# Modulation columns in the dense products: scaled by ScalarE and added up by GpSimd instead of summed by VectorE

## The reference, cut to what matters

```python
c_act = jax.nn.silu(c)
mod = c_act @ ada_w[layer] + ada_b[layer]          # (1, 2048) @ (2048, 6 * 2048)
sh1, sc1, g1, sh2, sc2, g2 = [m[:, None, :] for m in jnp.split(mod, 6, axis=-1)]
u = rms_norm(h, norm_mix_g[layer]) * (1.0 + sc1) + sh1
h = h + g1 * hybrid_mixer(u, ...)
u = rms_norm(h, norm_ffn_g[layer]) * (1.0 + sc2) + sh2
h = h + g2 * swiglu(u, ...)
```

## The kernel before, in words

| product | turns x groups | chunks of modulation columns a turn |
|---|---|---|
| in_1 | 8 x 8 | 1 |
| out_1 | 2 x 8 | 1 |
| ff_1 | 8 x 8 | 1 |
| ff_2 | 4 x 16 | 3 |
| out_2 | 2 x 8 | 2 |
| gate_up | 11 x 8 | 1, in its first 4 turns |
| down | 2 x 22 | none |

## Time and profile before

### The profile page before, as it was taken

The page is one execution under the profiler, slowest core; times in us unless marked ns, Lnnn a source line. Parts: engine busy times, 40 slices in busy tenths (PEclk is TensorE's granted clock), DMA queues, the critical chain, the costliest instruction groups (busy, mean ns, idle before and its releaser), DMA issues. The chain is left out here.

```text
span 3280.2 us, 57828 instructions
## 1 busy us (share of the span) xinstructions
PE 2891.9 (88%) x22235; PEld 2786.1 (85%) x22235; DVE 2000.5 (61%) x2742; ACT 1378.5 (42%) x2121; POOL 314.9 (10%) x427
## 2 busy tenths in 40 slices
PE   2399999769788999999999699999798999999998
PEld 2399998748788999988889588888688999999997
DVE  6856556746556666587788534545577654445664
ACT  1234334252434444444444334545434444444554
POOL 2011112600001111111111000000111100000000
PEclk6699999679898999999999788999999999999999
DMA  9688896110355877687788252324576765555553
GB/s 341 212 246 243 234 245 174 65 39 1 136 172 197 286 258 272 232 286 264 264 276 272 69 148 93 118 91 128 193 257 236 263 212 174 190 181 167 187 174 114
DMA packets 295455, 632.09 MB, mean 193 GB/s; under 512 B 23746, under 2 KB 44678, under 8 KB 295046
## 3 DMA queue, kind: packets, MB, share of 16 engines
q1 hardware_dynamic: 240080, 467.97, 44.5%
q0 software_dynamic: 43776, 159.40, 14.0%
q10 hardware_dynamic: 11446, 2.54, 0.5%
HBM read 627.77 MB, written 2.10 MB: 192 GB/s over the span
## 5 line engine op out<-in xcount | busy, mean ns | idle before, releaser
L741 PE MATMUL accumulators<-h_parts,weight_parts 128*128 128x256 f32 x5696 | 1454.7, 287 | 28.1 <-DVE weight_parts L679 27.9
L743 PE MATMUL accumulators<-h_parts,weight_parts 128*128 128x256 f32 x5696 | 1443.7, 285 | 0.0
L679 DVE TENSOR_TENSOR weight_parts<-weights,weight_parts 128x1024 fp32r<-128x1024 f32 (+1 forms) x840 | 877.6, 1058 | 532.8 <-ACT weight_parts L642 531.7
L741 PEld LDWEIGHTS accumulators<-h_parts,weight_parts 128*128 128x128 f32 x5696 | 1106.8, 194 | 44.6 <-DVE weight_parts L679 41.2
L743 PEld LDWEIGHTS accumulators<-h_parts,weight_parts 128*128 128x128 f32 x5696 | 1107.9, 195 | 0.0
L642 ACT ACTIVATE weight_parts<-weights 128x1024 fp32r<-128x1024 f32 (+1 forms) x840 | 747.3, 920 | 750.1 <-DMA weights<-in_w_in 201.9
L734 PE MATMUL accumulators<-h_parts,weight_parts 128*128 128x256 f32 x5696 | 935.6, 287 | 112.2 <-DVE h_parts L668 61.0
L734 PEld LDWEIGHTS accumulators<-h_parts,weight_parts 128*128 128x128 f32 x5696 | 798.0, 195 | 122.7 <-issue 89.3
L641 ACT ACTIVATE h_parts<-wide 128x512 fp32r<-128x512 f32 x216 | 135.6, 628 | 355.8 <-DMA weights<-in_w_ff 199.7
L362 DVE SCALAR_TENSOR_TENSOR ada_sums<-ada_weights,c_act,ada_sums 128x512 f32<-128x512 f32 x392 | 278.1, 746 | 0.0
L2177 DVE TENSOR_TENSOR in_weight_parts<-weights,in_weight_parts 128x512 fp32r<-128x512 f32 (+6 forms) x224 | 130.8, 597 | 209.2 <-ACT in_weight_parts L1964 208.1
(11 more groups left out here) (321 smaller groups left out, 1864.2 us busy)
## 6 DMA issues: line engine op xcount, KB each, us to landing
weights<-in_w_ff SPq DMA_DIRECT2D x128, 1024.0 KB, 6.5
weights<-in_w_in SPq DMA_DIRECT2D x80, 1024.0 KB, 8.1
h_t<-in_ada_w POOLq DMA_DIRECT2D x128, 512.0 KB, 5.9
ada_weights<-in_w_ada POOLq DMA_DIRECT2D x96, 512.0 KB, 6.2
weights<-in_ffn_w_gate SPq DMA_DIRECT2D x44, 1024.0 KB, 5.2
weights<-in_ffn_w_up SPq DMA_DIRECT2D x44, 1024.0 KB, 5.1
weights<-in_ffn_w_down SPq DMA_DIRECT2D x44, 1024.0 KB, 5.0
ada_weights<-in_w_ada SPq DMA_DIRECT2D x64, 512.0 KB, 8.2
```

The lines of the kernel that those rows point to most:

```text
L679: ins = nc.vector.tensor_tensor(w[:, held:held + take, 1, :], core.ring[:, q % RING, k:k + take, :], w[:, held:held + take, 0, :].bitcast( ...
L741: nc.tensor.matmul(accs[nt], w[:, held, 0, cols[nt]], xk[:, 1, :], start=False, stop=False, skip_group_check=True)
L743: ins = nc.tensor.matmul(accs[nt], w[:, held, 1, cols[nt]], xk[:, 0, :], start=False, stop=(last and nt % 2 == 1), skip_group_check=True)
```

## The change

`Ada.step` is used no longer in the dense products, only in the first phase. In its place ScalarE scales each row tile of columns, by one activation with the number as its scale (`Ada.scale`): the first two of a chunk into the two sums, the other 14 in place in the ring. The steps are placed behind ScalarE's high parts by the formula that placed them behind VectorE's low parts. GpSimd adds the 14 scaled tiles to the two sums in turn, then the sums to one another, and issues the loads in between, each when the slot has been added up (`Ada.loads_and_sums`). ScalarE's queue now holds the waits for landed columns and for taken sums. TensorE waits for the same semaphore `ada_sums_ready`, which GpSimd raises.

```diff
+    def scale(self, act, i, s):
+        nc, core, n = self.nc, self.core, self.per_turn
+        c, k = s // KT, s % KT
+        which = self.parts[c][1]
+        if s == 0:
+            act.wait_ge(core.ada_sums_taken, i * n + (self.chunks0 + 1))
+        q = c * AGROUPS + k // AK
+        if k % AK == 0:
+            act.wait_ge(self.landed[q % self.slots],
+                        i * (16 * self.per_slot) + 16 * (self.landed0 + q // self.slots + 1))
+        w = self.ring[:, q % self.slots, k % AK, :]
+        nc.scalar.activation(self.acc[:, c, k, :] if k < 2 else w, w, ACT.Copy,
+                             scale=core.c_act[:, KT * which + k:KT * which + k + 1]).then_inc(core.ada_scaled, 1)
+
+    def loads_and_sums(self, pool):
+        nc, core = self.nc, self.core
+        self.first_loads(pool)
+        chunks = self.turns * self.per_turn
+        for chunk in range(chunks):
+            acc = self.acc[:, chunk % self.per_turn]
+            scaled, added = self.scaled0 + KT * chunk, self.added0 + (KT - 1) * chunk
+            for k in range(KT):
+                w = self.ring[:, (chunk * AGROUPS + k // AK) % self.slots, k % AK, :]
+                pool.wait_ge(core.ada_scaled, scaled + k + 1)
+                if k >= 2:
+                    if k >= 4:
+                        pool.wait_ge(core.ada_added, added + k - 3)
+                    nc.gpsimd.tensor_tensor(acc[:, k % 2, :], acc[:, k % 2, :], w, ALU.add
+                                            ).then_inc(core.ada_added, 1)
+                load = chunk * AGROUPS + k // AK + self.slots
+                if k % AK == AK - 1 and load < chunks * AGROUPS:
+                    pool.wait_ge(core.ada_added, added + max(k - 1, 0))
+                    self.load(pool, load // (self.per_turn * AGROUPS), load % (self.per_turn * AGROUPS))
+            pool.wait_ge(core.ada_added, added + KT - 2)
+            nc.gpsimd.tensor_tensor(acc[:, 0, :], acc[:, 0, :], acc[:, 1, :], ALU.add).then_inc(core.ada_added, 1)
+            pool.wait_ge(core.ada_added, added + KT - 1)
+            pool.sem_inc(core.ada_sums_ready, 1)
...
                     nc.scalar.activation(w[:, held:held + take, 0, :], core.ring[:, q % RING, k:k + take, :], ACT.Copy
                                          ).then_inc(core.high_ready, take)
+                    if with_sums and 0 < q < st.unit - 1:
+                        n, slots, at = ada.per_turn * KT, KG * (st.unit - 2) // take, (KG * (q - 1) + k) // take
+                        for s in range(n * at // slots, n * (at + 1) // slots):
+                            ada.scale(act, i, s)
...
-                    if with_sums and 0 < q < st.unit - 1:
-                        n, slots, at = ada.per_turn * KT, KG * (st.unit - 2) // take, (KG * (q - 1) + k) // take
-                        for s in range(n * at // slots, n * (at + 1) // slots):
-                            ada.step(dve, i, s)
...
-                ada.first_loads(pool)
-                ada.other_loads(pool)
+                ada.loads_and_sums(pool)
```

51 lines of the change are left out of this document (28 added, 23 removed).

## The result

The changed kernel takes **3463.53 us** (median of 4 runs, 3457.72 to 3468.19), the kernel before 3285.14 us (4 runs, 3277.24 to 3285.92): ratio 1.0548, 95% interval 1.0522 to 1.0574, 178 us slower. The forecast was 3375 us with a range of 3300 to 3460. The direction was right, the size was not: the loss is about twice the forecast, and the time is 3.5 us above the range. The profiled execution took 3468.19 us, its span 3466.5 us, at a mean granted clock of 0.914 (before 0.929).

A forecast was written before the change was run, and what follows sets the result against it. TensorE was taken to bound ff_1 and gate_up, late weight loads behind VectorE's work ff_2. Terms of +46, +26, +12, +6 and +3 gave +93 on 3281.9, so 3375 us, range 3300 to 3460.

The forecast's parts named there:

- What bounds the kernel: TensorE alone in ff_1 and gate_up; in ff_2, weight loads that start late behind VectorE's low parts and sums.
- The loop of the earlier trace: In ff_2, weights landing, last low part (6.5 us), next load landing (7.2 us): 13.7 us for two groups, sums inside.
- Prices: Assumed costs per operation: ScalarE scaling 0.71 us, GpSimd addition 1.2 us, between 1.13 and 1.43.
- dear additions: Rival: GpSimd additions cost 1.43 us each, so late columns stop ScalarE and TensorE; +197 us, 3479 us, chance 0.12.
- The ring turns faster: Rival: no holding, additions at 1.13 us, weight loads start sooner in ff_2 and in_1; −16 us, 3266 us, chance 0.07.
- GpSimd yields: Rival: VectorE keeps the shared SBUF access and GpSimd waits without holding it; +30 us, 3312 us, chance 0.17.
- Held both ways: Claim that GpSimd's additions and VectorE's two-operand low parts each wait for the other's whole instruction on SBUF.
- Term 1, ff_2: Low parts and additions exclude each other, making a turn 119 us instead of 107.5; +46 us, ends −13 to +102.
- Term 2, out_2: GpSimd needs 58 us a turn against TensorE's 46.2, so TensorE waits for sums; +26 us, ends +7 to +40.
- Term 3, in_1: Held low parts lengthen the loop 0.6 us a group, partly made up by a shorter DMA queue; +12 us.
- Term 4, ff_1: VectorE's 5.3 us a group fits under TensorE's 5.77, except after relu steps; +6 us, ends 0 to +20.
- Term 5, out_1 and gate_up: Same shape as ff_1, in six turns; +3 us, ends 0 to +10.

The follow-up runs named there:

- e9: Kernel before, with VectorE's sum steps behind the group's last low part only in ff_2 and out_2: 3240.15 us, ratio 0.9879.
- e1: Changed kernel without GpSimd's additions, sums left out, ScalarE still scaling: 3284.51 us, ratio 1.0030 to the kernel before.
- e3: Changed kernel with each GpSimd addition replaced by a one-operand product by 1.0, sums left out: 3479.4 us, a single run.
- e2: Changed kernel with each GpSimd addition replaced by two fills that only write, sums left out: 3360.42 us, ratio 1.0241 to the kernel before.
- e10: Changed kernel with write-only fills for GpSimd's additions and TensorE's partition sums after the turn's last group: 3309.50 us, ratio 1.0074 to the kernel before.
- e4: Changed kernel with TensorE's partition sums after the turn's last group instead of ahead of it: 3422.84 us, ratio 1.0453 to the kernel before.
- e5: Changed kernel with each GpSimd addition waiting for the one just before it, opening gaps: 3470.35 us, ratio 1.0570 to the kernel before.
- e6: Changed kernel with VectorE making the additions at its old steps' places, GpSimd only loading: 3285.02 us, ratio 1.0009 to the kernel before.

## Why the prediction was right in kind and too small

**What bounds the kernel: right.** The loop of the earlier trace rows is real: e9 shortens it and gains 35 us in ff_2, if partly by faster loads. ff_1 and gate_up were covered by TensorE, and e1 shows that VectorE's freed time is worth nothing there.

**Prices: right.** Scaling 0.709 us (0.71 said). Addition 1.25 us alone, 1.31 at the median (1.2 taken, 1.13 to 1.43 as ends). The *dear additions* rival gave 3479 us, nearest to the measured 3463.5, but its cause did not occur: an addition by itself cost 1.25 us, not 1.43. That its time fits is luck. *The ring turns faster* fell with the low parts' means. *GpSimd yields* did not occur with the additions of the change; e3 shows it for another form.

**Held both ways: right.** Low parts of 128x1024 were to be about 1.8 us in mean with a minimum of 1.22; in ff_2 the mean is 1.98, over all stages 1.68. Additions that met one took up to 2.4 us, as said.

**Term 1, ff_2: slightly too small.** +61 for +46, within its ends. e2 and the changed kernel, 443.5 and 500.4 us, put 57 us on the held access; without holding ff_2 was to get shorter by 13, and e1 shows 6. What the term left out is in the last paragraphs of this section.

**Term 2, out_2: right.** +31 for +26. In the first turn TensorE waited 9.6 us for GpSimd's closing addition, as forecast; in the second it was stopped by the low part that eight additions held, before it came to the sums. e10 and e2 show a loss of the same order (+21, +38) with nothing held.

**Term 3, in_1: the first step that failed.** I took +12 of a computed +29, on the ground that part of a late start is made up by a shorter DMA queue. Measured: +40. Two things were wrong. The loop grew by more than the 1.2 us that I had computed (two slots share it, which gives the 0.6 us a group): from the first high part to the last low part, in groups with sums, 4.65 us before and 6.86 after, since the last high part comes 0.8 us later behind its scalings and the holds come on top. I had priced the two engines' work apart and taken the longer, and it stands in one chain. And less was made up than I took: from a last low part to the first high part that its slot's next load feeds, 9.43 us fell to 8.80, 0.6 of 2.2 us. The DMA share fell from 0.88 to 0.83, and TensorE's waits for VectorE appeared (21.6 us). e10, in which nothing is held and no sum is late, has in_1 at 429.3, so holding costs some 29 of the 40 us; the other 10 are open. Late sums cost nothing in this stage.

**Term 4, ff_1: the second step that failed.** "It fits, hidden under TensorE" is true of the low parts: TensorE waited for them for 4.5 us. I forgot that the sums have a deadline of their own, the matmuls ahead of the turn's last group, though I had written exactly that for out_2. In ff_1 the last scalings come in group 6, and the additions behind them, held by low parts, end 1.7 us after TensorE has run dry. +34 for +6, above its end of 20; e4 returns 24 us of it. By my own test ("if ff_1 lost more than 20 us, the cover would not exist") the cover was missing: for the sums.

**Term 5, out_1 and gate_up: missed in the same way.** +14 for +3, above its end of 10. TensorE waited for late sums there too (2.3 and 3.1 us); with the sums' matmuls later (e4) the two stages are at +1 and +5.

The forecast's sum lacks 93 us of the 186 by which the execution grew: 28 in in_1, 28 in ff_1, 15 in ff_2, 11 in out_1 and gate_up, 5 in out_2, the rest outside these stages.

**What no term held.** Two things. A low part waits for as many additions as follow one another, not for one; what that cost is not shown, since e5, which cuts the long holds, delays the sums. And pauses of TensorE are followed by stretches in which matmuls start 213 ns apart in place of 120. That adds about a third to the pauses (44 us on 121 in the table above), in all four stages. My terms priced waits alone.

The sum by cause, in shares of the 178 us: ScalarE's part, less what VectorE saves by it, about 0 (e1, e6). The shared access some 100 (the change less e2), 57 of it in ff_2, to 125 (e4 less e10). GpSimd's own time the rest, 80 by e2 and rather less in the change, since e2's fills are dearer than the additions. Late sums cost some 31 us, which lie in both: in ff_1 the holding acts by making the sums late, as e4 shows.

## What to carry to other kernels

Before work is moved to another engine, ask whether it costs by the engine's total or by its place in the queue. Here it was the place: putting it behind the instruction that releases the next transfer, as e9 did with two loops and no new engine, gained 1.2%. Two-operand additions on GpSimd beside two-operand subtractions on VectorE gave back all the time that they took off VectorE (476 us held for 456 us saved). And every result that an engine makes has a deadline of its own at its reader. It has to be priced in each stage, with the slower matmuls that follow a pause.

## What the runs showed of the hardware that I had not expected

- GpSimd keeps the shared access over additions that follow one another closely: eight of them in 9.92 us, and a VectorE subtraction beside them took 9.39 us in place of 1.22. With about 0.1 us between additions (e5) the longest was 2.99 us.
- GpSimd's product of a 128x512 tile by a constant took 1.48 us at best, its addition of two such tiles 1.25 us. VectorE was held much less by the product (mean 1350 ns against 1678). Why one operand is dearer than two stays open.
- Fills that only write (0.963 us for 1024 elements, 0.419 for 384) did not hold VectorE at all: 1221 ns on average over 584 low parts.
- In ff_1 each of seven pauses of 1.7 to 2.4 us was followed, one to two microseconds after TensorE had begun again, by about 3.4 us at a granted clock of 0.50, with TensorE busy all the time in the stretch shown.
